# First slabs of a three-layer network loaded and split two chunks at a time, and the first operands of two later mixers moved in the queues

## The reference

```python
# first block (16 meta tokens, then x)
a = rmsnorm(h, norm1);  proj = a @ w_in              # 21 columns of 128
y = [pool_mixer(u), forgetting_attention(...), stick_breaking_attention(...)]
h = h + concat(y) @ w_out
h = h + (silu(n(h) @ w_gate) * (n(h) @ w_up)) @ w_down;   h = rmsnorm(h, final_norm)
# layer 0: conformer convolution (4 chunks) beside block attention (8 heads), then an MLP
u = n(h) @ ab_w_in                                   # 20 columns of 128
h = h + concat([silu(layernorm(conv(glu))), attention(q, k, v)]) @ ab_w_out
h = h + square(relu(n(h) @ w_up)) @ w_down
# layer 1: gated linear recurrence, then an MLP
gate, xr = split(n(h) @ c_w_in)                      # 16 columns of 128
h = h + (rg_lru(conv(xr)) * gelu(gate)) @ c_w_out
h = h + square(relu(n(h) @ w_up)) @ w_down;          out = rmsnorm(h, final_norm)
```

## Time and profile before

| | |
|---|---|
| time, median of 3 runs | 949.3 us (948.92 to 950.01) |
| the profiled execution | 946.05 us |
| its span in the profile | 944.3 us, mean granted clock 0.987 |
| busy: PE, weight loads, DVE, ACT, POOL | 96%, 92%, 63%, 49%, 10% |
| DMA | 152.64 MB, mean 162 GB/s |

### The profile page before, as it was taken

The page is one execution under the profiler, slowest core; times in us unless marked ns, Lnnn a source line. Parts: engine busy times, 40 slices in busy tenths (PEclk is TensorE's granted clock), DMA queues, the critical chain, the costliest instruction groups (busy, mean ns, idle before and its releaser), DMA issues.

```text
span 944.3 us, 19567 instructions
## 1 busy us (share of the span) xinstructions
PE 908.0 (96%) x7460; PEld 871.1 (92%) x7460; DVE 590.8 (63%) x961; ACT 465.0 (49%) x733; POOL 92.0 (10%) x153
## 2 busy tenths in 40 slices
PE   8999898999999999999899999999998999999997
PEld 7988688999999998977799999999898999999996
DVE  4656345656666577545476666566888876655665
ACT  5445546543444355533564444444767654444443
POOL 4110000100000004920010000000212000000000
PEclk9999899999999999999899999999999999999999
DMA  7433112665555554732435555555444445555551
GB/s 243 167 115 132 45 68 91 223 201 186 182 181 185 199 180 133 239 104 78 151 135 200 178 181 192 185 196 179 136 152 144 172 157 179 194 185 193 181 178 45
DMA packets 44083, 152.64 MB, mean 162 GB/s; under 512 B 5764, under 2 KB 6020, under 8 KB 44036
## 3 DMA queue, kind: packets, MB, share of 16 engines
q1 hardware_dynamic: 40752, 146.36, 45.3%
q0 software_dynamic: 2912, 5.48, 1.9%
q10 hardware_dynamic: 372, 0.14, 0.1%
HBM read 148.58 MB, written 1.05 MB: 158 GB/s over the span
## 4 chain that ended last, share of the span: by engine, by line
PE 88%; DVE 6%; ACT 4%; issue 1%; DMA 1%; SPq 0%; DVEq 0%; ACTq 0%
PE bank L1188 26%; PE bank L1190 25%; PE bank L1189 25%; DVE alo L833 2%; PE bank L1496 2%; PE bank L1416 1%; PE bank L1272 1%; DVE wlo L808 1%; DVE h L843 1%; PE bank L1217 1%; ACT whi L427 1%; PE bank L1582 1%; PE bank L1289 1%; PE bank L1303 1%; DMA raw<-in_slabs 1%
## 5 line engine op out<-in xcount | busy, mean ns | idle before, releaser
L1188 PE MATMUL bank<-ahi,whi 128*128 128x256 f32 (+1 forms) x1416 | 407.2, 288 | 11.1 <-DVE alo L826 5.9
L1190 PE MATMUL bank<-ahi,wlo 128*128 128x256 f32 (+1 forms) x1416 | 400.5, 283 | 0.0
L1189 PE MATMUL bank<-alo,whi 128*128 128x256 f32 (+1 forms) x1416 | 400.5, 283 | 0.0
L808 DVE TENSOR_TENSOR wlo<-raw,whi 128x1024 fp32r<-128x1024 f32 x275 | 335.1, 1227 | 39.2 <-ACT whi L427 38.9
L427 ACT ACTIVATE whi<-raw 128x1024 fp32r<-128x1024 f32 x275 | 284.4, 1051 | 127.6 <-PE bank L1190 118.0
L1188 PEld LDWEIGHTS bank<-ahi,whi 128*128 128x128 f32 x1416 | 269.7, 190 | 14.7 <-DVE alo L826 7.0
L1189 PEld LDWEIGHTS bank<-alo,whi 128*128 128x128 f32 x1416 | 269.9, 191 | 0.4
L1190 PEld LDWEIGHTS bank<-ahi,wlo 128*128 128x128 f32 x1416 | 269.9, 191 | 0.0
L1188 PE MATMUL bank<-hidhi,whi 128*128 128x256 f32 x688 | 192.7, 280 | 0.9 <-DVE wlo L808 0.9
L1189 PE MATMUL bank<-hidlo,whi 128*128 128x256 f32 x688 | 192.4, 280 | 0.0
L1190 PE MATMUL bank<-hidhi,wlo 128*128 128x256 f32 x688 | 192.3, 280 | 0.0
(11 more groups left out here) (184 smaller groups left out, 711.1 us busy)
## 6 DMA issues: line engine op xcount, KB each, us to landing
raw<-in_slabs SPq DMA_DIRECT2D x275, 512.0 KB, 3.3
shared<-zpad POOLq DMA_DIRECT2D x64, 35.5 KB, 3.1
shared<-in_convw POOLq DMA_DIRECT2D x4, 512.0 KB, 7.2
h<-in_xT SPq DMA_DIRECT2D x4, 272.0 KB, 4.4
vtok<-in_gatew POOLq DMA_DIRECT2D x2, 512.0 KB, 4.0
out<-y SPq DMA_DIRECT2D x4, 256.0 KB, 2.7
par<-in_par ACTq DMA_DIRECT2D x1, 72.0 KB, 3.4
poolw<-in_poolw ACTq DMA_DIRECT2D x1, 64.0 KB
```

The source lines that it names most:

```text
L808: dve.tensor_tensor(wlo[:, n % R, :, :], raw[:, n % R, :, :], whi[:, n % R, :, :].bitcast(F32), ALU.subtract).then_inc(lo_done, 1)
L1188: pe.matmul(dst, hi, xh, start=start, stop=False, skip_group_check=True)
L1189: pe.matmul(dst, hi, xl, start=False, stop=False, skip_group_check=True)
L1190: return pe.matmul(dst, lo, xh, start=False, stop=stop, skip_group_check=True)
```

## The change

**Start.** SP issues only the first part of x, then slabs 0 and 1 in four pieces each (two chunks, 128 x 256 floats, 128 KB), piece by piece for both, then slabs 2 and 3. ACT issues the other three parts of x behind `par`. ACT and DVE split, chunk pair by chunk pair, the operand and the two pieces; PE starts a chunk pair when its pieces are done. The warm-up has 16 products, not 24. The split of slab 2 goes ahead of the squares. The sums of squares (`stats`) go behind column 2; column 3 gets a bank of its own (`acc_bank[0]`), and the waits for free banks are weaker up to column 5.

**Layer 0's mixer.** At u = 12 ACT splits the first row operand ahead of the transposes' copy, where it came at the end of the step; DVE takes its rest first thing in step 12, with the slab that was split at u = 11 behind it. The layernorm products (four of L1069) go ahead of the last `take`. The copy of the transposed values (L668) goes ahead of the exponentials in every fourth step, and PE waits for it before row 0.

**Layer 1's mixer.** The step sizes, square roots, gelus and the first two recurrences come one or two columns earlier; the first two row operands go to `hidhi` and `hidlo`, which no column reads, so they need not wait for the last column; an operand's rest is taken before the next `gated_output`.

```diff
-WARM_UP = 24
+WARM_UP = 16
+PIECES = KC // 2
...
+        def in1_bank(i):
+            return acc_bank[0] if i == 3 else col_bank(i)
...
+        piece_loaded = [[sem(f"piece_loaded{b}_{i}") for i in range(PIECES)] for b in range(2)]
+        piece_hi, piece_lo = sem("piece_hi"), sem("piece_lo")
...
+        def row_operand(s, k):
+
+            if s == A_LRU and k < 2:
+                return hidhi[:, k, :], hidlo[:, k, :]
+            return ahi[:, k, NMETA:], alo[:, k, NMETA:]
...
         @block.sync
         def _(sp):
-            for c in range(0, KC, 2):
-                sp.dma_start(h[:, c:c + 2, :], xT[:, c:c + 2, :]).then_inc(x_loaded[c // 2], 16)
-            for s in range(R):
+            sp.dma_start(h[:, 0:2, :], xT[:, 0:2, :]).then_inc(x_loaded[0], 16)
+            for i in range(PIECES):
+                for b in range(2):
+                    sp.dma_start(raw[:, b, 2 * i:2 * i + 2, :], slabs[b][:, 2 * i:2 * i + 2, :]).then_inc(piece_loaded[b][i], 16)
+            for s in range(2, R):
                 sp.dma_start(raw[:, s, :, :], slabs[s]).then_inc(raw_loaded[s], 16)
...
             act.dma_start(par[:, 0:PAR_N], par_in).then_inc(par_loaded, 16)
+            for c in range(2, KC, 2):
+                act.dma_start(h[:, c:c + 2, :], xT[:, c:c + 2, :]).then_inc(x_loaded[c // 2], 16)
             act.dma_start(fbias[:, :], fbias_in).then_inc(small_loaded, 16)
...
             act.wait_ge(par_loaded, 16)
-            residual_hi(N_NORM1, 0)
-            split(0)
-            split(1)
+            for i in range(PIECES):
+                act.wait_ge(x_loaded[i], 16)
+                for k in (2 * i, 2 * i + 1):
+                    g = GAIN[N_NORM1] + k
+                    act.activation(ahi[:, k, :], h[:, k, :], ACT.Copy, scale=par[:, g:g + 1]).then_inc(ahi_ready, 1)
+                for b in range(2):
+                    act.wait_ge(piece_loaded[b][i], 16)
+                    act.activation(whi[:, b, 2 * i:2 * i + 2, :], raw[:, b, 2 * i:2 * i + 2, :], ACT.Copy)\
+                       .then_inc(hi_done if i == PIECES - 1 else piece_hi, 1)
+            split(2)
             squares(0)
-            split(2)
             split_early(IN1)
...
@@ -657,22 +679,23 @@
                 if u in IN2_STEP or u in OUT2_STEP:
                     split_ahead(n)
                     n += 1
+                if u == max(IN2_STEP) + 1:
+                    act.wait_ge(slab_used, OUT2)
+                    operand_hi(A_CAT2, F_CAT2, CAT2_STEP[u])
                 if u % 2 == 0:
                     if 1 <= u // 2 <= MOBA_S:
                         transposed(u // 2 - 1, FOX_S, moba_copies)
+                    if u % 4 == 0 and u < MOBA_U:
+                        pair = u // 4
+                        act.wait_ge(vT, 7 + pair)
+                        act.activation(vtok[:, 0:2, P * pair:P * pair + P],
+                                       acc_bank[2][:, 0:2 * P].rearrange("p (g d) -> p g d", g=2), ACT.Copy).then_inc(v_ready, 1)
                     if u // 2 < MOBA_S:
                         probabilities(u // 2, FOX_S, MOBA_N)
-                if u % 4 == 0 and u < MOBA_U:
-                    pair = u // 4
-                    act.wait_ge(vT, 7 + pair)
-                    act.activation(vtok[:, 0:2, P * pair:P * pair + P],
-                                   acc_bank[2][:, 0:2 * P].rearrange("p (g d) -> p g d", g=2), ACT.Copy).then_inc(v_ready, 1)
...
-                if u == max(IN2_STEP) + 1:
-                    act.wait_ge(slab_used, OUT2)
...
-                if u in CAT2_STEP:
+                if u in CAT2_STEP and u > max(IN2_STEP) + 1:
                     operand_hi(A_CAT2, F_CAT2, CAT2_STEP[u])
...
-                if i in (12, 13):
-                    j = 4 * (i - 12)
+                if i in (11, 12):
+                    j = 4 * (i - 11)
                     act.wait_ge(lru_m2, j + 4)
                     act.activation(sq[:, j:j + 4, NMETA:], sq[:, j:j + 4, NMETA:], ACT.Sqrt, scale=-1.0)\
                        .then_inc(lru_root, 4)
-                if i == 14:
-                    gelus(0, 3)
-            act.wait_ge(slab_used, OUT3)
+                if i in (13, 14):
+                    gelus(3 * (i - 13), 3 * (i - 12))
             for j in range(KC):
+                if j == 2:
+                    act.wait_ge(slab_used, OUT3)
                 operand_hi(A_LRU, F_LRU, j)
                 split_ahead(OUT3 + j - 1)
-                if j == 0:
-                    gelus(3, 6)
                 if j == 1:
                     gelus(6, KC)
...
 
                 dve.wait_ge(ahi_ready, KC * s + k + 1)
-                dve.tensor_tensor(alo[:, k, NMETA:], af[:, k, :], ahi[:, k, NMETA:].bitcast(F32), ALU.subtract)\
-                   .then_inc(alo_ready, 1)
+                hi, lo = row_operand(s, k)
+                dve.tensor_tensor(lo, af[:, k, :], hi.bitcast(F32), ALU.subtract).then_inc(alo_ready, 1)
...
-            for k in range(KC):
-                residual_lo(N_NORM1, A_NORM1, k, 0)
-            for n in range(LOOKAHEAD):
-                split(n)
+            for i in range(PIECES):
+                for b in range(2):
+                    if i < PIECES - 1:
+                        dve.wait_ge(piece_hi, 2 * i + b + 1)
+                    else:
+                        dve.wait_ge(hi_done, b + 1)
+                    w = (slice(None), b, slice(2 * i, 2 * i + 2), slice(None))
+                    dve.tensor_tensor(wlo[w], raw[w], whi[w].bitcast(F32), ALU.subtract)\
+                       .then_inc(lo_done if i == PIECES - 1 else piece_lo, 1)
+                for k in (2 * i, 2 * i + 1):
+                    residual_lo(N_NORM1, A_NORM1, k, 0)
+            split(2)
             split_early(IN1)
...
             for n in range(IN1 + 1, IN1 + FOX_READY + 1):
-                take(n, col_bank(n - IN1), n - IN1 - 1, in1_scale(n - IN1 - 1), in1_lo(n - IN1 - 1))
+                take(n, in1_bank(n - IN1), n - IN1 - 1, in1_scale(n - IN1 - 1), in1_lo(n - IN1 - 1))
...
             for u in range(MOBA_U + 3):
 
+                if u == max(IN2_STEP) + 1:
+                    operand_lo(A_CAT2, CAT2_STEP[u])
+                    split_ahead(OUT2 - 1)
                 softmax_slot(u, MOBA_S, FOX_S, MOBA_N, alibi_bias)
+                if u == LN_VAR_STEP + 1:
+                    dve.wait_ge(ln_std, 1)
+                    for k in range(CONV_C):
+                        dve.tensor_tensor(cv[:, k, :], cv[:, k, :], r1[:, :], ALU.mult).then_inc(ln_norm, 1)
                 if u in IN2_STEP:
                     c = IN2_STEP[u]
-                    take(n, acc_bank[n % 2], c, QSCALE if 8 <= c < 12 else 1.0)
+                    take(n, acc_bank[n % 2], c, QSCALE if 8 <= c < 12 else 1.0, ahead=n < OUT2 - 1)
                     n += 1
                 if u in OUT2_STEP:
                     split_ahead(n)
                     n += 1
-                if u in CAT2_STEP:
+                if u in CAT2_STEP and u > max(IN2_STEP) + 1:
                     operand_lo(A_CAT2, CAT2_STEP[u])
...
-                if u == LN_VAR_STEP + 1:
-                    dve.wait_ge(ln_std, 1)
-                    for k in range(CONV_C):
-                        dve.tensor_tensor(cv[:, k, :], cv[:, k, :], r1[:, :], ALU.mult).then_inc(ln_norm, 1)
             for i in range(max(CAT2_STEP.values()) + 1, KC):
                 operand_lo(A_CAT2, i)
                 split_ahead(OUT2 + i)
...
             for i, c in enumerate(IN3_ORDER):
-                take(IN3 + i, col_bank(i), c, ahead=IN3 + i < OUT3 - 1)
+                take(IN3 + i, col_bank(i), c, ahead=IN3 + i < OUT3 - 1 and i != 10)
+                if i == 10:
+                    decay_steps(range(4))
+                    split_ahead(IN3 + i)
...
-                if i in (11, 12):
-                    decay_steps(range(4 * (i - 11), 4 * (i - 10)))
-                if i == 13:
-                    recur(0)
+                if i == 11:
+                    decay_steps(range(4, KC))
+                if i in (12, 13):
+                    recur(i - 12)
 
             def gated_output(j):
                 dve.wait_ge(lru_gelu, j + 1)
                 dve.tensor_tensor(af[:, j, :], t8[:, j, :], proj[:, j, NMETA:], ALU.mult).then_inc(af_ready, 1)
             gated_output(0)
-            recur(1)
             for j in range(KC):
+                operand_lo(A_LRU, j)
                 if j + 1 < KC:
                     gated_output(j + 1)
-                operand_lo(A_LRU, j)
                 split_ahead(OUT3 + j - 1)
                 if j + 2 < KC:
                     recur(j + 2)
...
-                slab_ready(n + 1)
+                if n > IN1:
+                    slab_ready(n + 1)
                 for k in range(KC):
+                    if n == IN1 and k % 2 == 0:
+                        if k < KC - 2:
+                            pe.wait_ge(piece_lo, k + 2)
+                        else:
+                            slab_ready(n + 1)
...
```

(11 more changed lines are left out.)

11 lines of the change are left out of this document (4 added, 7 removed).

## The result

The changed kernel takes **938.07 us** (median of 4 runs, 936.2 to 939.78) against 949.11 for the kernel before beside it (4 runs, 946.52 to 950.01). The ratio is 0.9888, 95% interval 0.986 to 0.9915: about 11 us faster. The prediction was 939.0, range 935.5 to 944.0.

A forecast was written before the change was run, and what follows sets the result against it. PE was taken to bound the kernel, with 88% of the chain of waits; gains of 3.5 (start), 5.4 (layer 0) and 1.4 (layer 1) sum to 10.3 us, taking the median from 949.3 to 939.0, range 935.5 to 944.0.

The forecast's parts named there:

- Start: Start of the kernel: first columns end 4.1 us earlier, at 15.9; gain taken as 3.5 us (1.0 to 5.0).
- two bounds: Start: PE's last pair begins at 12.0 if the data are there, about 13.6 if ACT is held up twice.
- lower bound of 12.0: Start: PE begins its last pair at 12.0 us, if the data are there in time.
- dear pieces: Rival at the start: a packet costs 0.16 us whatever its size, first columns end at 21.8, total 944.3; chance 0.06.
- a low clock: Rival at the start: last burst and 16 products behind it run low, end 18.3, gain 1.7, total 940.8; chance 0.2.
- a bandwidth for each queue: Start: had each queue its own bandwidth, the gain would be 5 us instead of 3.5; no chance given.
- Layer 0's mixer: Layer 0's output rows: row 0 starts 3.2 us earlier and takes 3.0, row 1 starts 5.4 us earlier; gain 5.4.
- Layer 1's mixer: Layer 1's output rows: first rest at 724.9 instead of 725.96, rows then at DVE's pace; gain 1.4 us.
- the list of DVE's work behind the new wait: Layer 1's mixer: from 712.4 DVE's slabs, takes, steps, recurrences and gated output sum to 11.5 us, ending at 723.9.
- one vanishing: Clock: the fall at 107.9 (2 to 3 us) vanishes, total 936.5.

The follow-up runs named there:

- one queue: The changed kernel with x loaded from SP's queue again, each pair of chunks ahead of its two pieces of the slabs: 937.07 us, ratio 0.9883.
- ten fillers: The kernel before with ten products of ones that nobody reads put into PE's pauses, nothing of the change: 945.53 us, ratio 0.9961.

## Why the prediction was right, and where it was not

**Start: right, and for its reasons.** The forecast had the first pair of pieces complete at 7.1 (7.18; the first of the two was there by 5.97), the last pair at 12.9 (12.82), the first columns' end at 15.9 (15.93), POOL's sums done at about 19 (18.58), the sums of squares without a wait at 18.77. ACT was held up twice, as worked out, for 0.81 and 0.18 us, and a pair without a wait took it 1.44 us and not 1.58. The forecast's 12.9 was the middle between two bounds and not a result of its own, so that it came within 0.1 is luck in part; the lower bound of 12.0 is what one queue reaches (11.89). The warm-up ended at 7.29 and not at 6.2: until about 6 us PE shows 6 or 7 records in a us (two a product), behind that 10, and the forecast had taken the mean of all 24 products. Why the first ones are slower, at a PEclk of 1.00 by the rows, is open. It cost nothing, as the first pair came at 8.10. The term was 0.55 us too small: it left room for products at the low level, and PEclk stayed 1.00 here in after and in every kernel with the new start. The rivals of dear pieces (21.8) and of a low clock (18.3) are out, and so is that of a bandwidth for each queue: the engines moved as much with one queue as with two (353 and 352 GB/s), and the second one cost 0.9 us.

**Layer 0's mixer: right.** In before's time, that is with the 0.71 us added by which the values are early, row 0 starts at 447.72 (forecast 447.75) and takes 3.0 us at the full level, row 1 starts at 451.59 (451.65), and the 1.48 us ahead of row 3 stay. 5.42 us against 5.4, and 5.45 with this part alone.

**Layer 1's mixer: wrong in size, 0.2 instead of 1.4 us.** The step that failed is the list of DVE's work behind the new wait, priced by rows in which POOL was silent. In before's time (6.04 us added) the decays ended at 712.8 and not 712.4, slab 13 took 1.55 and not 1.13 and slab 14 1.22, the second four decays 1.75 and not 1.42; column 13 started at 714.75 and not 714.0. These are 0.4, 0.42, 0.1 and 0.33 us, 1.2 in all, and the first rest was there at 726.0 and not 724.9, where before it was there at 725.96. The prediction read 0.716 us a square from a row that stood for eight squares, six of 0.61, one of 0.74 and one of 1.60 beside a slab: the lengthening was already in that row and was averaged away. The runs with the decays behind the slab and without POOL's squares show the mechanism and its size. The wait for the squares itself was in the forecast; what they do to DVE's work beside them, and it to them, was not. PE's remaining wait of 2.16 and DVE's 2.99 us a row came as forecast.

**The clock: right in sign, not foreseen in place.** The forecast counted on each fall of before staying where it was, or one vanishing. The one at 449 vanished as stated, that at the start too; that at 108 was 6.8 us longer in the profiled run and cost, with a new one at 142.6, 3.4 us of time. This lies inside the range. It is not the change's doing: the parts that leave the start alone had 13.7 us there as well, and on the kernel before ten fillers win 3.7 us at the same place. The terms as measured in the traces, 4.05 + 5.42 + 0.22 = 9.7, stand against 11.0 us between the medians, whose interval reaches from 8 to 13 us. The two traces are only 6.3 us apart in device time because the profiled run of before was 3.1 us under its median, at a clock of 0.987 where most of its runs have 0.983 to 0.985, and that of after 1.7 us over its own, at 0.989 against 0.992 to 0.994. Where the runs without a profile had their low stretches is not on record.

**Luck.** The median's forecast was 0.9 us too high, closer than its terms deserve. The term of layer 1 was 1.2 us too large and that of the start 0.55 too small, which alone would have made the forecast 0.6 too low; the clock, which no term held, turned that round.

## What to carry to other kernels

Before moving DVE work into a stretch where POOL is active, look for the least and the most of POOL's durations and not only the mean: one long instruction among equal ones shows what sharing costs, and it falls on both engines. Put a wait for another engine behind the work that does not need it, not ahead of it. Where a latency-bound stretch leaves PE with pauses of 0.5 to 2.5 us, products of ones that nobody reads can be worth more than the pause: ten of them won 3.7 us in the kernel before (2.4 to 5.0) and 3.4 between the medians in the changed one.

## What was not expected of the hardware

- The low level at one and the same place in the program lasts 6.8 us in one profiled run and 10.2 or 13.7 in another, with the code ahead of it unchanged (A to B takes 52.2 to 54.4 us in kernels with one low stretch there), and it can begin while PE is busy: in after PE was busy 1.52 of the 2 us ahead of 98, and all of 98 to 99.
- A low stretch costs little where PE waits for DVE anyway: 24.6 to 24.7 us from row 0 to the next stage without one, 24.9 to 25.1 with one of 3.4 us.
- A square of 0.61 us on POOL takes 0.79 beside DVE's decays and 1.59 beside a slab's subtraction; the decay goes from 0.41 to 0.82, the slab from 1.22 to as much as 1.63.
- Two queues with the engines full (352 and 353 GB/s) were 0.9 us worse than one, by the order in which x and the pieces arrived.
